# Attention values computed by column halves, row sums spread before the second transposes, and the final norm taken through PSUM

## What is computed

```python
def plain_attention(q, k, v):
    s = jnp.einsum('bqhd,bnhd->bhqn', q, k).astype(jnp.float32) * (HEAD_DIM ** -0.5)
    p = jax.nn.softmax(s, axis=-1).astype(v.dtype)
    return jnp.einsum('bhqn,bnhd->bqhd', p, v)
...
def diff_attend(q, k, v, lam_val):
    B, Q = q.shape[:2]
    s = jnp.einsum('bqhd,bnhd->bhqn', q, k).astype(jnp.float32) * (HEAD_DIM ** -0.5)
    p = jax.nn.softmax(s, axis=-1).reshape(B, DIFF_HEADS, 2, Q, -1)
    p = p[:, :, 0] - lam_val * p[:, :, 1]
    return jnp.einsum('bhqn,bnhd->bqhd', p.astype(v.dtype), v)
...
def swa_sink_attention(x, w_qkv, sinks, w_o, cos, sin):
    ...
    probs = jax.nn.softmax(jnp.concatenate([scores, sink], axis=-1), axis=-1)[..., :-1]
    out = jnp.einsum('bnhgqk,bnkhd->bnqhgd', probs.astype(v.dtype), vb)
    return out.reshape(bsz, s, A_HEADS * A_HEAD_DIM) @ w_o
...
def first_block(x, c, ctx, c_ctx, ada_w, ada_b, norm_g, w_in_ab, w_out_ab, diff_lambda, diff_sub_g,
              na_rpb, w_in_c, w_out_c, attn_sinks, ffn_w1, ffn_w3, ffn_w2, final_g):
    ...
    return rmsnorm(x, final_g)
...
    mem_k, mem_v = jnp.split(mem @ mem_w_kv, 2, axis=-1)
```

## Time and profile before

| | us |
|---|---|
| median of 3 runs | 2727.66 (2725.49 to 2730.65) |
| the profiled execution | 2737.28 |
| its span | 2735.4 |
| PE busy | 2628.6, 96% |
| DVE / ACT / POOL busy | 48% / 54% / 67% |
| stages a0t, a3t | 30.1, 31.7 |

### The profile page before, as it was taken

How to read it: one execution, slowest core, us unless ns; L and a number is a source line. 1 busy time by engine, 2 the same in 40 slices (tenths; PEclk the granted TensorE clock), 3 DMA queues, 4 the chain that set the end, 5 groups by cost and what they waited for, 6 DMA issues and landing times.

```text
span 2735.4 us, 49579 instructions
## 1 busy us (share of the span) xinstructions
PE 2628.6 (96%) x17698; PEld 2393.9 (88%) x17698; DVE 1308.6 (48%) x2950; ACT 1488.5 (54%) x2562; POOL 1826.2 (67%) x770
## 2 busy tenths in 40 slices
PE   7999999999999999999999999999999999999998
PEld 5898779989987899988989998889979899989897
DVE  5216543353374443335465565455543555563655
ACT  5327744445454554444565566565545655555655
POOL 0447748878875788863578855498645688535885
PEclk7999999999999999999999999999999999999998
DMA  6325425555543555542345544355433455323553
GB/s 232 116 77 193 157 98 185 185 176 184 184 156 128 186 179 184 185 147 78 124 162 185 186 136 131 109 193 188 146 105 124 147 184 186 130 78 124 179 187 133
DMA packets 115634, 421.68 MB, mean 154 GB/s; under 512 B 12832, under 2 KB 14112, under 8 KB 114976
## 3 DMA queue, kind: packets, MB, share of 16 engines
q1 hardware_dynamic: 115200, 417.00, 45.3%
q10 hardware_dynamic: 288, 2.62, 0.3%
HBM read 418.52 MB, written 1.05 MB: 153 GB/s over the span
## 4 chain that ended last, share of the span: by engine, by line
PE 48%; POOL 24%; issue 20%; DVE 4%; ACT 2%; DMA 1%; POOLq 0%; SPq 0%; ACTq 0%; DVEq 0%
POOL ring_low L2479 24%; PE bank L1030 10%; PE bank L635 9%; PE bank L620 5%; PE bank L621 5%; PE bank L622 5%; PE bank L629 3%; PE bank L630 3%; PE bank L915 2%; PE bank L946 1%; PE bank L785 1%; PE bank L793 1%; PE bank L964 1%; DVE scr L1822 1%; ACT ring_high L1278 1%
## 5 line engine op out<-in xcount | busy, mean ns | idle before, releaser
L2479 POOL TENSOR_TENSOR ring_low<-ring,ring_high 128x1024 fp32r<-128x1024 f32 x766 | 1826.0, 2405 | 887.5 <-ACT ring_high L1278 715.3
L1030 PE MATMUL bank<-rounded,ring_high 128*128 128x512 f32 x2296 | 575.6, 392 | 2.9 <-DVE qt L2086 2.9
L635 PE MATMUL bank<-rounded,ring_low 128*128 128x256 f32 (+1 forms) x3540 | 535.9, 287 | 0.3 <-POOL ring_low L2479 0.3
L1496 ACT ACTIVATE ring_high<-ring 128x1024 fp32r<-128x1024 f32 x448 | 469.7, 1051 | 94.5 <-DMA ring<-in_units 92.5
L635 PEld LDWEIGHTS bank<-rounded,ring_low 128*128 128x128 f32 x3540 | 493.5, 191 | 28.6 <-POOL ring_low L2479 0.5
L1030 PEld LDWEIGHTS bank<-rounded,ring_high 128*128 128x128 f32 x2296 | 412.9, 189 | 78.1 <-issue 3.9
L1278 ACT ACTIVATE ring_high<-ring 128x1024 fp32r<-128x1024 f32 x337 | 350.7, 1052 | 96.6 <-DMA ring<-in_units 96.0
L620 PE MATMUL bank<-hid_high,ring_high 128*128 128x256 f32 x1232 | 350.6, 285 | 9.1 <-DVE hid_low L2128 5.5
L622 PE MATMUL bank<-hid_high,ring_low 128*128 128x256 f32 x1232 | 350.0, 284 | 0.0
L621 PE MATMUL bank<-hid_low,ring_high 128*128 128x256 f32 x1232 | 349.9, 284 | 0.0
L629 PE MATMUL bank<-rounded,ring_high 128*128 128x256 f32 (+1 forms) x1076 | 293.4, 305 | 3.0 <-ACT ring_high L1278 1.7
(11 more groups left out here) (235 smaller groups left out, 3891.0 us busy)
## 6 DMA issues: line engine op xcount, KB each, us to landing
ring<-in_units SPq DMA_DIRECT2D x785, 512.0 KB, 3.3
xt<-in_x SPq DMA_DIRECT2D x2, 1024.0 KB, 9.3
nbias<-in_bias ACTq DMA_DIRECT2D x1, 1536.0 KB, 7.0
vt<-in_mem ACTq DMA_DIRECT2D x1, 1024.0 KB, 6.5
out_x<-xt SPq DMA_DIRECT2D x8, 128.0 KB, 1.7
consts<-in_consts SPq DMA_DIRECT2D x1, 832.0 KB, 9.5
cols<-in_cols SPq DMA_DIRECT2D x1, 639.0 KB, 5.5
consts<-in_consts SPq DMA_DIRECT2D x1, 512.0 KB, 6.3
```

Source lines behind the costliest of these rows:

```text
L635: return pe.matmul(out, w[1], x[0], start=False, stop=stop)
L1030: one = pe.matmul(both_of(b), unit(u, k * P, P)[0], hi_lo(k, stream), start=(k == 0), stop=False)
L1496: act.activation(whole(ring_high, u), whole(ring, u), ACT.Copy).then_inc(unit_high, 1)
L2479: pool.tensor_tensor(whole(ring_low, u), whole(ring, u), whole(ring_high, u).bitcast(fp32), ALU.subtract).then_inc(unit_ready, 1)
```

## The change

1. **Values.** Items whose heads are 64 wide are `paired`: the 8 neighbourhood items, 8 of at1, 8 of a0t and 8 of a3t. V (128 keys x 64 columns) is now the stationary operand and the transposed probabilities (256 or 128 queries) the moving one; head a writes partitions 64a to 64a+63 of the output bank, so the output is feature-major at once and `out_t` goes. Since the queries are now columns, the reciprocals of the row sums have to be spread over the partitions: `rows` does it with four matmuls (a reciprocal column broadcast to 64, times the identity) into a bank of `turn_plan`, ACT copies it to SBUF (`rows_out`), and DVE multiplies the output in its bank. `rows` stands on PE ahead of the second transposes; in `turn_plan` it stands between the first and the second, and DVE's reciprocals and `out_low(s - 1)` move up to just behind the modulations. ACT's `out_high(s - 1)` moves ahead of `out_pt(s, 0)`. In an item of at1, `fill(5 * s + 3)` stands ahead of the values instead of in their middle.
2. **Sink sums.** The row sum and the sink's exponential stand in pairs, and one reduction adds them; the factor lambda of the differential items is folded into a later instruction.
3. **Final norm.** The inverse goes to PSUM bank 7 and the eight multiplications read it there. The high and low parts of x take another slot (s=1), so ACT's `high_of` no longer waits for the memory's last values; DVE does values 0 and 1, then `low_of`, then values 2 to 7. The projections of a0 read the other slot.
4. **NORMED.** Tiles 4 to 7 come after tile 21 instead of tile 20.

```diff
-NORMED = {PEELED[0]: range(0, 4), PEELED[1]: range(4, KD)}
+NORMED = {PEELED[0]: range(0, 4), PEELED[2]: range(4, KD)}
...
             order = []
             for s, d in enumerate(items):
-                order += [(s, n) for n in range(len(fulls(d)))]
-                if s and not items[s - 1]["diff"]:
+                half = len(fulls(d)) // 2
+                order += [(s, n) for n in range(half)]
+                if paired(d):
+                    order.append((s, "rows"))
+                order += [(s, n) for n in range(half, len(fulls(d)))]
+                if not paired(d) and s and not items[s - 1]["diff"]:
                     order.append((s - 1, "ot"))
...
+                    def rows(s):
+
+                        b = turn_bank(s, "rows")
+                        pe.wait_ge(*when(st, "rc", s))
+                        for i in range(2):
+                            for a in range(2):
+                                mm = pe.matmul(banks[b][64 * a:64 * a + 64, P * i:P * (i + 1)],
+                                               four(RC, s)[:, 2 * i + a:2 * i + a + 1].broadcast_to([P, 64]),
+                                               const("ident", P), start=True, stop=True)
+                        mm.then_inc(*mark(out_t_ready, st, "rows", s))
+                        reader[b] = (st, "rows_out", s)
+
+                    def values_paired(s):
...
+                        blocks = d["nk"][1] // P
+                        for j in range(blocks):
+                            for a in range(2):
+                                x = probs_by_key(d, a, j)
+                                first = 0 if j < d["nk"][0] // P else P
+                                mm = pe.matmul(banks[b][64 * a:64 * a + 64, first:T], d["heads"][a]["v"](j), x,
+                                               start=(j == 0), stop=(j == blocks - 1), skip_group_check=True)
...
+                        mm.then_inc(*mark(attn_ready, st, "attn", s))
+                        reader[b] = (st, "o", s)
...
+                        if paired(items[s]):
+                            rows(s)
                         transposes(s, 1)
...
+                    def rows_out(s):
+
+                        act.wait_ge(*when(st, "rows", s))
+                        act.activation(o_sb(s, 0, T), banks[turn[s, "rows"]][:, 0:T], ACT.Copy
+                                       ).then_inc(*mark(act_done, st, "rows_out", s))
...
                     for s in range(last + 1):
+                        if s and paired(items[s - 1]):
+                            out_high(s - 1)
                         out_pt(s, 0)
                         ada_rest(5 * s)
                         ada_rest(5 * s + 1)
+                        if paired(items[s]):
+                            rows_out(s)
                         if shallow:
                             exps(s + 1, 0)
                         out_pt(s, 1)
-                        if s:
+                        if s and not paired(items[s - 1]):
                             out_high(s - 1)
...
-                act.wait_ge(*when("mem", "v", 7))
-                high_of("last1", "value", lambda k: X(k, 0))
+                high_of("last1", "value", lambda k: X(k, 0), s=1)
...
-                            link(dve.tensor_tensor(four(SM, s), four(SM, s), four(ES, s), ALU.add))
-                        if n == 2:
-                            link(dve.reciprocal(four(RC, s), four(SM, s)))
+                            link(dve.tensor_reduce(four(RC, s).rearrange("p (i a) -> p i a", a=2), sum_pairs(s), AX.X, ALU.add))
+                            link(dve.reciprocal(four(RC, s), four(RC, s)))
...
+                        if paired(d):
+                            dve.wait_ge(*when(st, "rows_out", s))
+                            dve.tensor_tensor(b[:, 0:T], b[:, 0:T], o_sb(s, 0, T), ALU.mult
+                                              ).then_inc(*mark(dve_done, st, "onorm", s))
+                            return
...
+                        if paired(items[s]):
+                            reciprocals(s)
+                        if s and paired(items[s - 1]):
+                            out_low(s - 1)
                         if shallow:
                             lowest(s + 1, 0)
                         out_pt(s, 1)
...
-                norm("last1", D, EPS_RMS)
+                norm("last1", D, EPS_RMS, inverse=banks[7][:, 0:T])
...
-                evacuate_v("mem", 8, lambda n: mem_v(n % 2, 256 * (n // 2), 256 * (n // 2) + 256))
-                low_of("last1", "x", lambda k: X(k, 0))
...
+                values_mem(range(0, 2))
+                low_of("last1", "x", lambda k: X(k, 0), s=1)
+                values_mem(range(2, 8))
```

More of the change, by code:

```diff
@@ L956, in out_t @@
                         d = items[s]
-                        if d["diff"]:
+                        if d["diff"] or paired(d):
                             return
@@ L1409, in out_high @@
                         d = items[s]
-                        if not d["diff"]:
+                        if paired(d):
+                            act.wait_ge(*when(st, "onorm", s))
+                            act.activation(tiles_in("high", d), in_bank(out_bank(s, shallow), 1), ACT.Copy
+                                           ).then_inc(*mark(act_done, st, "ohigh", s))
+                        elif not d["diff"]:
                             act.wait_ge(*when(st, "ot", s))
```

66 lines of the change are left out of this document (50 added, 16 removed).

## The result

| | before | after |
|---|---|---|
| median of 12 runs each, us | 2731.31 | 2751.72 |
| lowest to highest | 2720.23 to 2744.53 | 2742.53 to 2759.60 |
| profiled execution, its span | 2737.28, 2735.4 | 2742.53, 2740.8 |

The changed kernel is slower: ratio 1.0070, 95% interval 1.0055 to 1.0086, which is +15 to +23 us. The forecast was +2.8. The time lies in its wide range, which ends at 2758, but not in its own narrow one, 2722 to 2739. The two traces alone are only 5.4 us apart, and this has two reasons. The traced execution of the changed kernel is the fastest of its twelve, and in the trace of before the first attention stage begins 8.8 us later behind code that the change doesn't touch.

The account below looks back on a forecast made before the run. PE (TensorE) was taken to bound the kernel, busy 2628.6 of 2735.4 us. Terms -17.1 + 15.4 + 5 - 0.5 + 0 = +2.8 on 2727.66 gave 2730.5 us; 8-in-10 range 2715 to 2758, own narrow range 2722 to 2739.

Parts of the forecast that it names:

- serial rival: Column halves work one after another: values and rows cost at1 +0.93 us an item; total 2760 us, chance 0.18.
- The loop in a0t and a3t: Second transposes wait for ACT's copy, closing a 5.04 us loop against 3.27; a0t +8.5, a3t +6.9, sum +15.4 us.
- Clock: PE gaps in a0t and a3t lower its granted clock; between 0 and +12 us, taken as +5.
- the rival of the costlier loop: Half clock through both a0t and a3t (+12 instead of +5) and gated closing steps +3 to +5; about 2742 us, chance 0.12.
- Column halves at the same time: The two column halves overlap as row halves do; in at1 values take 2.06 us and rows 0.78.
- the rule set beside it in the prediction: Trainium skill rule: weight loads overlap running matmuls only when the row group differs; by it the serial sum would hold.
- The serial sum: Per item of at1 with column halves one after another: 1.78 more and 0.35 more for shape changes, giving +0.93 us.
- Values in at1: Cheaper values and dropped output transposes, less the added rows: -1.25 us an item, -10.0 for 8 items.
- at0: Four neighbourhood items save 1.25 us each, four context items 0.3 each, the last output transpose 0.9.
- Final norm: Products end 8 to 9 us earlier, but a 4 to 7 us gap before n=6 replaces the wait; -0.5 us.
- NORMED: After tile 21 the hid_low wait goes and another comes before the next stage; 0 us (-3 to +2).
- Sinks: Sink sums by one reduction instead of an addition, in a0t and a3t: 0 us.

Follow-up runs that it names:

- The first run: The changed kernel with the new path left out of a0t and a3t; median 2726.81 us, ratio 0.9984 to the kernel before.
- the four behind it: Cumulative on the changed kernel in a0t and a3t: reciprocals' bank, early reciprocals, old out_high/out_low places, later rows (plus two repairs elsewhere); 2734.25, 2737.27, 2728.58, 2710.44 us.
- the reordered version: Column halves in at0 and at1 only, norming after tile 20, six value groups first, plus ACT's modulation-row copy ahead of its group's last feed; 2707.75 us, ratio 0.9906.
- two versions with the same instructions there: Norming after tile 20, six value groups first; column halves in at0 and at1 only (2720.63 us), or all 32 items with mended orders (2710.44 us).
- The second repair: On top of the run with reciprocals in the output bank, VectorE makes item s+1's reciprocals ahead of the minima of s+2; 2737.27 us, ratio 1.0022.

## Why the prediction was right and wrong

- **The number**: +20.4 for +2.8. That the wide range holds it is luck. It reaches to 2758 only because it takes in half of the serial rival (2752 to 2766), and that rival fell. By the total alone 2751.72 would even be taken for it; only the traces tell the two apart. What was right is the sign, and that slower had the largest chance, 0.43. The error lies mostly in two terms: the values in at1, and NORMED.
- **The loop in a0t and a3t**: right in mechanism and size. 5.04 was worked out, 5.08 came; the stretches with the clock's share are +10.8 and +10.9 for +11.0 and +9.4. The first run shows that the loss is there, the four behind it that it comes from the orders. They show three orders behind it, though, and the forecast named two. It had the bank order and the place of `out_high`. "the reciprocals lie beside it" was wrong: in a0t `rows` waits up to 0.99 an item for them. ("It waits for reciprocals that DVE makes long before", which was said of at1, holds there: all 14 waits of that kind stand in a0t and a3t.) With the bank wait gone they hold the item at 4.26. It didn't show in the sum, because the bank's wait behind it was the longer one.
- **Clock**: taken at +5, and about that came. In the changed kernel two of the six steps of a0t are 8.06 and 6.17 for 5.08; with 1.9 for the fed units, 2.2 are left for half clock. In a3t three steps are 5.91, 8.06 and 6.17, which leaves 3.0. Not every stretch at half clock costs: item 2 to item 3 of a0t (1263.04 to 1268.13) is at 0.50 until 1266.7 and takes 5.09 all the same, since PE waits there. The windows over the two stages have a mean clock of 0.88 and 0.84, in the earlier trace rows 0.94 and 0.89. So of the rival of the costlier loop the half clock through both stages (+12) did not come, and its closing steps at +3 to +5 did (NORMED below).

```profile
1248.00:1290.60 42.60, 30.36 (x235) 19.41 (x236) 21.43 (x86) 22.70 (x86) 4.66 (x2) 0.88 0.07 26
2391.00:2434.00 43.00, 31.45 (x232) 19.70 (x228) 21.55 (x86) 22.67 (x86) 4.66 (x2) 0.84 0.07 26
```

- **Column halves at the same time**: right; the serial rival fell, and the rule set beside it in the prediction is not borne out for column halves: records of the two start 6 ns apart, and weight loads of 0.14 us find room inside steps of 0.216. The values take 1.88 to the next instruction and `rows` 0.59. To both comes 0.09 ahead of them: the step from the last 512-column record to the first one with 64 columns is 0.32, where such records follow each other at 0.23. That makes 1.97 for 2.06 and 0.68 for 0.78, so the 0.35 for a change of shape was taken too large by 0.1. (The serial sum has a slip of 0.05 an item, 0.93 for 0.88; nothing hangs on it.)
- **Values in at1**: the term that was mis-sized. "I take -1.25, for 8 items -10.0" came out as -0.85 an item and -4.0 for the stage with its output projection (from its first scores to the next FFN). PE's own instructions gave what was worked out and 0.2 more, by which an item would be 10.84; it was 11.44 with PE's wait for the modulation rows (0.51 by the profile, 0.59 from start to start), and 10.85 when ACT's order took that away. One item took 0.56 more than the others. The forecast had counted PE's parts and not asked what of ACT comes sooner when PE is faster: the rows are ready at the same time behind two feeds, and PE comes earlier. Behind the stage, PE's wait for `ring_low` is 1.70 where it was 0.2: a part of the gain went to the supply of weights. That wait stands in the reordered version too.
- **at0**: -7.1 forecast; -6.4 in the run with NORMED put back, which is this term alone (-5.8 and -4.8 in two versions with the same instructions there).
- **Final norm**: "A gap of 4 to 7 with its clock stretch takes the place of the one removed" is what came: 6.59, by the chain that was named. The sum, -0.5, came out as +0.9 (from PE's wait of 1.5 us ahead of the memory's keys, at 1162.79 before and at 1147.36 after, to the first scores of a0t), inside -2.1 to +1.5. The forecast also gave -7.3 if the wait didn't arise; with six value groups first it is -6.7.
- **NORMED**: "I take 0 for both together (-3 to +2)" was wrong, +3.9. The forecast saw that the wait moves to the closing `gated_ffn`; it set 2.7 against 2.7, and it was 3.81 and 4.01. The step that failed is that it took the new wait to be as long as the old one because the DVE work is the same 8 us, and did not set PE's remaining work against it: behind tile 21 that is 4.84 us, as worked out above for the first FFN.
- **Sinks**, and the modulation products moved in front of the values: 0 was taken for both. No run tries either apart; they are inside the terms above.

The sum of the errors is 0.7 (at0) + 7.3 (at1 to a0t) + 3.9 (NORMED) + 1.3 (a0t and a3t) = 13.2, and 2.8 + 13.2 = 16.0, each of them from one trace. The rest to the 20.4 between the medians is not explained by the two traces: of the changed kernel's twelve executions the traced one is the fastest, with a mean clock of 0.977 where the others have 0.971 to 0.976, so more half clock in the others is likely, but they have no trace.

## What to carry to other kernels

When an edit puts a new product into a chain of engines, write down for every instruction that it adds or moves what stands ahead of it in its own queue, and follow the loop until it closes: here the item went from 5.08 to 4.26, 4.45, 3.97 and 3.61 us as three orders and one of my own were mended in turn. The second repair by itself gained nothing, since another wait took its place. Only the longest was visible at a time, and each repair showed the next. And when a step on the bounding engine gets shorter, look at once for what its neighbours had ready just in time; the gain is worth only what their queues let through, and a swap of two lines of ScalarE was worth 0.6 us in each of most items of at1 here (11.44 to 10.85), and some 7 us in the two stretches around it. And work that is put behind the last product of a stage is covered only by what PE has left to do there.

## What the runs showed of the hardware

Matmuls with 64 stationary columns in the two column halves run side by side: two records start 6 ns apart and a pair of 256 columns goes through in 0.216 us, as one record of full width does in 0.215. With one half's eight records first in the queue, PE starts the other half's work along with the fifth of them. Each change between 128 and 64 stationary columns costs PE about 0.09 us in at1: the start-to-start step is 0.32 where it is 0.23 without a change, and 0.31 where it is 0.216. The weight loads pause for 0.36 us there ahead of such a block and for 0.38 behind it, mostly with nothing named but issue.

VectorE's instructions with all operands in SBUF can last as long as the GpSimd instruction that they meet. In the run with six value groups first, four of the eight low parts (128x256) began while GpSimd was in a `ring_low`. They ended 0.3 us behind it and took 1.15 to 2.62 us; the four that began while it stood still took 0.41. In before, five of the eight products of the final norm took 1.89 to 2.62 in this way and three 0.47. With the factor in PSUM all eight took 0.48 beside the same `ring_low`. This is what the final norm's edit gains from.

```profile
1204.68 2.62 DVE L1960 TENSOR_TENSOR rounded<-xt,rounded 128x256 fp32r<-128x256 f32 x1
```
